# Adding the old scan state in PSUM with unit-matrix products instead of on VectorE

## The reference, cut to what matters

```
def step(state, inp):
    r_t, w_t, k_t, v_t, kk_t, a_t = inp
    sa = jnp.einsum('bhvk,bhk->bhv', state, -kk_t)
    state = (state * w_t[:, :, None, :] + sa[..., None] * (kk_t * a_t)[:, :, None, :]
             + v_t[..., None] * k_t[:, :, None, :])
    return state, jnp.einsum('bhvk,bhk->bhv', state, r_t)
```

## Time and profile before

| What | Value |
|---|---|
| Median of 3 runs | 2411.03 us |
| The profiled execution, its own time | 2415.91 us |
| Its span in the trace | 2414.1 us |
| PE busy | 2265.8 us (94%) |
| PEld busy | 1705.2 us (71%) |
| DVE busy | 1255.7 us (52%) |
| ACT busy | 934.1 us (39%) |
| POOL busy | 830.2 us (34%) |
| Mean granted clock of TensorE | 0.974 |

### The profile page before, as it was taken

The page is one execution under the profiler, slowest core; times in us unless marked ns, Lnnn a source line. Parts: engine busy times, 40 slices in busy tenths (PEclk is TensorE's granted clock), DMA queues, the critical chain, the costliest instruction groups (busy, mean ns, idle before and its releaser), DMA issues.

```text
span 2414.1 us, 46358 instructions
## 1 busy us (share of the span) xinstructions
PE 2265.8 (94%) x19576; PEld 1705.2 (71%) x19576; DVE 1255.7 (52%) x2027; ACT 934.1 (39%) x1665; POOL 830.2 (34%) x456
## 2 busy tenths in 40 slices
PE   8999999999978998888888899999998999999998
PEld 6886778888866647777777747877887766763476
DVE  5028254022164576777777515695313899736123
ACT  4238434233244433444444423464323222344133
POOL 2310334344313115444444203344441433430246
PEclk9999999999979998999999999999997999999999
DMA  4312222232302210000000122244221333222232
GB/s 143 118 51 78 70 70 88 94 99 86 105 25 78 96 42 3 10 10 10 10 10 10 38 70 70 96 183 133 94 87 63 129 113 114 87 87 79 70 90 84
DMA packets 49883, 180.71 MB, mean 75 GB/s; under 512 B 5600, under 2 KB 5856, under 8 KB 49440
## 3 DMA queue, kind: packets, MB, share of 16 engines
q1 hardware_dynamic: 46064, 166.89, 21.4%
q10 hardware_dynamic: 3632, 11.08, 1.2%
HBM read 167.39 MB, written 10.55 MB: 74 GB/s over the span
## 4 chain that ended last, share of the span: by engine, by line
PE 72%; issue 12%; DVE 7%; ACT 4%; POOL 3%; DMA 1%; POOLq 0%; ACTq 0%; SPq 0%; DVEq 0%
PE ps L596 15%; PE ps L597 15%; PE ps L598 15%; PE ps L599 6%; POOL ring_lo L2224 3%; PE ps L858 2%; PE ps L897 2%; PE ps L644 2%; PE ps L1093 1%; PE ps L888 1%; PE ps L925 1%; PE ps L715 1%; PE ps L730 1%; PE ps L705 1%; PE ps L1036 1%
## 5 line engine op out<-in xcount | busy, mean ns | idle before, releaser
L2224 POOL TENSOR_TENSOR ring_lo<-ring,ring_hi 128x1024 fp32r<-128x1024 f32 x232 | 566.0, 2448 | 1018.3 <-ACT ring_hi L1150 1018.2
L598 PE MATMUL ps<-u_lo,ring_hi 128*128 128x512 f32 x968 | 384.7, 397 | 0.0
L1150 ACT ACTIVATE ring_hi<-ring 128x1024 fp32r<-128x1024 f32 x232 | 243.3, 1053 | 113.2 <-DMA ring<-in_wall 109.9
L599 PE MATMUL ps<-arena,ring 128*128 128x512 f32 x608 | 266.1, 594 | 6.4 <-ACT arena L1595 3.3
L599 PEld LDWEIGHTS ps<-arena,ring 128*128 128x128 f32 x608 | 114.4, 190 | 154.3 <-issue 138.6
L596 PE MATMUL ps<-mlp_u_hi,ring_hi 128*128 128x512 f32 x512 | 204.9, 400 | 12.3 <-DVE u_lo L1712 8.2
L598 PEld LDWEIGHTS ps<-u_lo,ring_hi 128*128 128x128 f32 x968 | 183.8, 190 | 43.5
L596 PE MATMUL ps<-mid_hi,ring_hi 128*128 128x512 f32 x512 | 203.3, 397 | 2.6 <-POOL ring_lo L2224 2.6
L597 PE MATMUL ps<-mlp_u_hi,ring_lo 128*128 128x512 f32 x512 | 203.6, 398 | 0.0
L598 PE MATMUL ps<-mid_lo,ring_hi 128*128 128x512 f32 x512 | 202.5, 396 | 0.0
L597 PE MATMUL ps<-mid_hi,ring_lo 128*128 128x512 f32 x512 | 202.5, 395 | 0.0
(11 more groups left out here) (425 smaller groups left out, 4331.0 us busy)
## 6 DMA issues: line engine op xcount, KB each, us to landing
ring<-in_wall SPq DMA_DIRECT2D x273, 512.0 KB, 3.6
s_tables<-arena ACTq DMA_DIRECT2D x16, 512.0 KB, 2.8
arena<-s_tables SPq DMA_DIRECT2D x16, 512.0 KB, 3.6
arena<-bias_lines SPq DMA_DIRECT2D x16, 448.0 KB, 4.3
arena<-in_lora SPq DMA_DIRECT2D x8, 384.0 KB, 3.1
h<-in_x SPq DMA_DIRECT2D x1, 2048.0 KB, 8.1
out<-arena ACTq DMA_DIRECT2D x8, 256.0 KB, 2.9
consts<-in_consts SPq DMA_DIRECT2D x1, 1216.0 KB, 14.4
```

Source lines behind the costliest of these rows:

```text
L598: return nc.tensor.matmul(y, w_hi, low, start=False, stop=x == k - 1)
L599: return nc.tensor.matmul(y, ring[:, at:at + P], rhs(x), start=x == 0, stop=x == k - 1)
L1150: nc.scalar.activation(ring_hi[:, slot], ring[:, slot], ACT.Copy).then_inc(sem("weights_high"), 1)
L2224: G.tensor_tensor(ring_lo[:, slot], ring[:, slot], ring_hi[:, slot].bitcast(F32), ALU.subtract).then_inc(sem("weights_split"), 1)
```

## The change

After L1014 of steps 1 to 6, each product L1023 gets another one ahead of it: the unit matrix (weights, `const("eye")`) times the old state, into bank `C`, which it overwrites (`start=True`). L1036 of these steps then adds to `C` instead of overwriting it. VectorE scales bank `C` once by `decay`, in one tensor_scalar, and that is the new state; the products `st_p`, their tile and their semaphore are gone.

```
@@ PE, in the scan's step, for d, for e
+                                if j < NCH - 1:
+                                    nc.tensor.matmul(C[d][rows, 0:CH], const("eye", 0, CH)[rows, :], s_sb_rw[j % 2][d][rows, :],
+                                                     start=True, stop=False)
                                 nc.tensor.matmul(O[d][rows, at], s_sb_rw[j % 2][d][rows, :], F[d]["ro"][rows, at],
                                                  start=True, stop=False)
...
                                 mm = nc.tensor.matmul(C[d][e * HEAD:(e + 1) * HEAD, 0:CH], F[d][("ka", "be")[e]][:, at],
-                                                      v_u[e][:, at], start=True, stop=True)
+                                                      v_u[e][:, at], start=j == 0, stop=True)
@@ DVE, in the scan's step
                         new, added = s_sb_rw[(j + 1) % 2][d], bank(4 * d + 2, CH)
-                        if j == 0:
-                            ins = TS(new, added, decay, None, ALU.mult)
-                        else:
-                            dve.wait_ge(sem("state_decayed"), n(12, k - 1))
-                            ins = STT(out=new, in0=added, scalar=decay, in1=st_p[d], op0=ALU.mult, op1=ALU.add)
-                        ins.then_inc(sem("state_ready"), 1)
-                    if j < NCH - 2:
-                        for d in range(2):
...
-                            TS(st_p[d], s_sb_rw[(j + 1) % 2][d], p_end[parity][d][:, nxt_c:nxt_c + 1], None, ALU.mult
-                               ).then_inc(sem("state_decayed"), 1)
+                        TS(new, added, decay, None, ALU.mult).then_inc(sem("state_ready"), 1)
```

More of the change, by code:

```diff
@@ L385, in program @@
         o_sb, dev = beside[2:4], beside[4:6]
-        st_p = [take(CH) for _ in range(2)]
         p_end = [[take(NCH) for _ in range(2)] for _ in range(2)]
```

## The result

The changed kernel takes 2420.54 us, the median of 6 runs (2419.36 to 2429.57), against 2410.9 us for the kernel before (median of 6, 2409.7 to 2422.31). The ratio is 1.0038, 95% interval 1.0022 to 1.0054: slower by 5 to 13 us, some 9 us in the middle. The forecast was 2418, a ratio of 1.0029.

A forecast was written before the change was run, and what follows sets the result against it. TensorE's stream was taken to bound the scan: +10.7 us for the unit products less 3.8 us back from VectorE makes +6.9, on the median 2411.0 some 2418 us (+0.29%); range for 8 in 10, 2412 to 2426.

The forecast's parts named there:

- The stream of TensorE sets the pace of the scan: Full scan steps: TensorE's products set the 2.67 us step, while VectorE and ScalarE answer during L1023 and the filler.
- Four products cost 0.23 us: Steps 1 to 6 of the scans: four unit products priced like L1023, 0.23 us in each of 45 steps, 10.4 us.
- the prediction's own sign (more than 0.5): Scan steps: prediction wrong if the unit products' group takes more than 0.5 us where L1023 took 0.23.
- rival A: Unit and `ro` products: the order costs overlap, 0.35 to 0.46 us per step, 2424 to 2429 us; chance 0.30.
- The argument that issue reaches past waiting records: Unit and `ro` products: from L888's 16 ns a record, head 1 is not held up by head 0's waiting records.
- The last pair's late steps pay 0.10: Last pair, steps 4 to 6: 0.13 us of slack leaves 0.10 us to pay in each, 0.3 us together.
- VectorE gives back 3.8 us: Scan steps: without L2083, whose instructions stretched beside GpSimd, TensorE's waits for late copies go, 3.8 us back.
- Nothing else is late: Scan steps after the change: no other work comes late, since VectorE gets to the copies 0.4 us earlier; 0 us.
- The sum, +6.9 us: Whole kernel: +10.7 us for the unit products less 3.8 us from VectorE, giving 2418 us.
- Rival B: Full steps: copies L2061 and L1522 really hold L1036, so unit products cost nothing; 2407 us; chance 0.13.
- Rival C: Half-clock stretches, up to 3.4 us each, may go or come; 0.05 that two cancel the main case's loss alone.
- the one stretch that the prediction allowed before it called itself wrong: Outside the scans: prediction wrong if the time there moves by more than a clock stretch, up to 3.4 us.

The follow-up runs named there:

- The half alone: VectorE's half: the changed kernel without the unit products, what was L1036 always overwriting; ratio to the kernel before 0.9965 (0.9953 to 0.9977).
- the half alone: TensorE's half: the kernel before plus unit products written to unused columns of bank C, result not used; ratio 1.0064 (1.0049 to 1.0079).

## Why the prediction was right

Its direction, place and mechanism held, and the time lay 2.5 us above the forecast.

- *The stream of TensorE sets the pace of the scan.* Right: products added there make the step longer by their own time (2.956), products taken out of it make it shorter (2.446), and the same products in free quarters leave it at 2.68.
- *Four products cost 0.23 us.* This term was mis-sized. It is 0.281 in 45 steps, 12.6 us instead of 10.4. The group takes 0.51 us where L1023 took 0.23, and by the prediction's own sign (more than 0.5) this choice was wrong, though by one round and not by rival A's 0.35. The quarters' own time is 0.233, as with alternating heads (2.908); 0.048 is one round that head 1 lags. The argument that issue reaches past waiting records held in the main: rival A's 0.35 to 0.46 did not come. It missed that the reach is not free at the seam. A strict program order of matmuls, which the page "TensorE: Matmul & The Clock Gate" of the Trainium skill states (Part 3, The mechanism), would have given the rival's 0.35 to 0.46. This trace does not agree: the step grew by 0.281, and head 1's unit product starts ahead of head 0's `ro` product. The 0.46 was itself reckoned from 5 record times for the old group, which shows 4 (0.23 us).
- *The last pair's late steps pay 0.10.* They pay 0.15 (2.397 against 2.245), 0.5 us together, since the group is longer by the same round.
- *VectorE gives back 3.8 us.* Right: 3.6 in the steps of the changed kernel. The half alone confirms it in the steps (3.7).
- *Nothing else is late.* Wrong by one place: the wait for issue, 1.4 us in the last pair. The sum by the steps is 12.6 + 0.5 - 3.6 + 1.4 = +10.9, inside the ratio's interval of 5 to 13. The two traces give 10.4, since the last pair before had a disturbed step too: 3.001 us where 2.534 was due, 0.5.
- *The sum, +6.9 us.* By the steps it was 3.5 us short: 2.2 for the unit products, 0.9 for the wait for issue and 0.4 for the rest. That the median came out only 2.5 us over the forecast lies within the noise; the sum is not confirmed to the microsecond.
- *Rival B, the products hide.* Refuted by the half alone, 1.0064.
- *Rival C, the clock.* Stretches at half clock did move between profiled executions, ahead of the scans and in them. The one that the prediction priced at up to 3.4 us cost 1.7 in its step. Outside the scans the trace after is 4.7 us shorter, 4.1 of it ahead of the first scan. That is more than the one stretch that the prediction allowed before it called itself wrong; there the granted clock was 0.55 before and 0.91 after, in the same 19 us, so I do not read it as a sign against the scans' account, though no run isolates it. That is why spans of single profiles (+4.0) say less than the steps and the medians.

## What to carry to other kernels

Count what an engine that sets the pace gets, not what an idle engine loses: 384 short records on TensorE outweighed the 96 instructions that VectorE lost, and their stalls. Before giving up such an addition, look which quarters of the array the neighbours use: the same products cost 0.28 us a step behind products of their own quarters and at most 0.005 beside products of the others, and the larger gain was to move work that was already there. A stall between VectorE and GpSimd can go with one instruction: here it was enough to take the one that has both operands in SBUF to an idle engine (ratio 0.9978).

## What the runs showed of the hardware

- The four 64x64 quarters of the array keep their own pace of 58 ns for each fp32 record. A product of a free quarter starts ahead of one that stands before it in the program and whose quarter is busy; the seam costs one round of about 50 ns (0.048 us a step).
- VectorE's tensor_scalar from SBUF to SBUF took 241 ns alone and up to 1325 ns beside GpSimd; the same form with PSUM as input stayed at 283 to 285 ns.
- Instructions arrive in 16 KB packets through the DMA engines. Beside four 512 KB loads no packet came for 8.4 to 9.4 us, and in four kernels TensorE stood still for 1.2 to 1.8 us; in two of these half clock followed, in the other two (the changed kernel among them) it did not. With the loads later, tested in one kernel, it did not stand still.
